# All output gates projected in the mixing stage, modulation rows turned as they come, and two buffers for high parts of weights

## What is computed

```python
mod = silu(c) @ ada_w + ada_b                    # 6 x 1024 per sequence: sh1, sc1, gt1, sh2, sc2, gt2
h = rms(x, norm1_w) * (1 + sc1) + sh1
proj = h @ w_in                                  # inputs, output gates g_z h_g s_z m_o, and 4 x 1024 gates
out_a = rms(gated_delta(g_qkv, ...)) * silu(g_z)   # branch A, width 256, and its new states
out_b = rms(hgrn2(h_q, h_f, h_i, ...)) * silu(h_g)
out_c = rms(ssd(s_xbc, s_dt, ...) * silu(s_z))
out_d = rms(mlstm(m_q, m_k, m_v, ...)) * sigmoid(m_o)
x = x + gt1 * (sum over branches n of sigmoid(gate_n) * (out_n @ w_branch_n)) @ w_out
x = x + gt2 * swiglu(rms(x, norm2_w) * (1 + sc2) + sh2)
y = rms(x, final_norm_w)
```

## Time and profile before

| what | value |
|---|---|
| median of 3 runs | 1264.69 us (1263.65 to 1268.71) |
| the profiled execution's own time | 1261.61 us |
| its span, first to last instruction | 1259.8 us |
| TensorE busy | 1166.7 us, 93% |
| VectorE busy | 576.5 us, 46% |
| ScalarE busy | 397.4 us, 32% |
| mean granted TensorE clock | 0.955 |
| moved by DMA | 116.76 MB, mean 93 GB/s |

### The profile page before, as it was taken

The page is one execution under the profiler, slowest core; times in us unless marked ns, Lnnn a source line. Parts: engine busy times, 40 slices in busy tenths (PEclk is TensorE's granted clock), DMA queues, the critical chain, the costliest instruction groups (busy, mean ns, idle before and its releaser), DMA issues. The chain is left out here.

```text
span 1259.8 us, 26885 instructions
## 1 busy us (share of the span) xinstructions
PE 1166.7 (93%) x11789; PEld 1091.8 (87%) x11789; DVE 576.5 (46%) x1054; ACT 397.4 (32%) x545; POOL 11.6 (1%) x29
## 2 busy tenths in 40 slices
PE   5679889999998898999999999959999999999997
PEld 3478888887767788999999998959999999999996
DVE  1365877678668663433333345452222222453322
ACT  1344383741102215932222221152232322341121
POOL 0000110000000000000000000000000000000000
PEclk9779999999779888999999999979999999999998
DMA  9802621122466306263333221213233232233301
GB/s 303 272 3 68 121 70 35 36 69 86 153 202 167 74 3 154 70 132 105 84 84 86 82 89 49 68 34 101 68 99 91 75 100 58 67 96 88 93 1 72
DMA packets 191034, 116.76 MB, mean 93 GB/s; under 512 B 36650, under 2 KB 189351, under 8 KB 190678
## 3 DMA queue, kind: packets, MB, share of 16 engines
q1 hardware_dynamic: 190358, 115.16, 32.8%
q0 software_dynamic: 576, 0.14, 0.1%
HBM read 108.31 MB, written 6.96 MB: 92 GB/s over the span
## 5 line engine op out<-in xcount | busy, mean ns | idle before, releaser
L833 PE MATMUL ps<-high_parts,scr_parts 128*128 128x272 f32 x2848 | 551.8, 293 | 16.7 <-DVE hT_parts L2765 7.9
L833 PEld LDWEIGHTS ps<-high_parts,scr_parts 128*128 128x128 f32 x2848 | 454.5, 191 | 20.1 <-issue 8.7
L833 PE MATMUL ps<-hT_parts,scr_parts 128*128 128x272 f32 x1488 | 414.2, 291 | 0.0
L2662 DVE TENSOR_TENSOR scr_parts<-ring,scr_parts 128x1024 fp32r<-128x1024 f32 (+1 forms) x104 | 133.7, 1286 | 331.4 <-ACT scr_parts L1826 328.2
L833 PEld LDWEIGHTS ps<-hT_parts,scr_parts 128*128 128x128 f32 x1488 | 276.9, 190 | 0.0
L1826 ACT ACTIVATE scr_parts<-ring 128x1024 fp32r<-128x1024 f32 (+1 forms) x104 | 115.2, 1109 | 467.4 <-PE ps L833 467.0
L833 PE MATMUL ps<-pj_parts,scr_parts 128*128 128x272 f32 x992 | 166.5, 292 | 2.1 <-DVEq L1966 1.8
L833 PE MATMUL ps<-high_parts,wx_hi 128*128 128x272 f32 x416 | 130.9, 315 | 20.4 <-DVE hT_parts L2035 7.3
L833 PEld LDWEIGHTS ps<-pj_parts,scr_parts 128*128 128x128 f32 x992 | 140.5, 188 | 3.6 <-DVEq L1966 2.2
L833 PE MATMUL ps<-high_parts,ring_parts 128*128 128x272 f32 x416 | 124.0, 298 | 0.0
L833 PE MATMUL ps<-hT_parts,wx_hi 128*128 128x272 f32 x416 | 123.9, 298 | 0.0
(11 more groups left out here) (326 smaller groups left out, 1060.9 us busy)
## 6 DMA issues: line engine op xcount, KB each, us to landing
ring<-in_w_in_dram SPq DMA_DIRECT2D x62, 512.0 KB, 5.5
ring<-in_ada_w_dram SPq DMA_DIRECT2D x48, 512.0 KB, 6.6
ring<-in_ffn_w_in_dram SPq DMA_DIRECT2D x44, 512.0 KB, 5.1
ring<-in_ffn_w_out_dram SPq DMA_DIRECT2D x16, 384.0 KB, 3.6
ring<-in_ffn_w_out_dram SPq DMA_DIRECT2D x16, 320.0 KB, 4.1
ring<-in_w_out_dram SPq DMA_DIRECT2D x8, 512.0 KB, 6.2
x_scratch<-scr SPq DMA_DIRECT2D x1, 2176.0 KB, 13.6
scr<-x_scratch SPq DMA_DIRECT2D x1, 2176.0 KB, 14.8
```

The costliest lines, as they stand in the source:

```text
L833: return pe.matmul(out, lhsT, rhs, start=start, stop=stop, skip_group_check=True)
L2662: dve.tensor_tensor(lo, src, hi.bitcast(F32), SUB).then_inc(w_split, 1)
```

## The change

- Groups 3 and 7 go into the mixing order, which ends 8, 3, 7, 14; `Z_ORDER` is empty, so `M_GATE` is 0 and the projection stage begins with the gate pieces. The tiles of group 3 wait in the plan for gdn's last sample state, those of group 7 for hgrn's, and in `read_group` for their write-outs. Lifting starts at piece 8 instead of 12.
- The first four gate loads wait for the four late groups, the others for the split of the piece that held their slot.
- Tiles with an odd number, but not the last, put their high parts into `pj[MO]`, `pj[MO + 1]` (the place of the last group's result); a copy then waits for the tile two back.
- A block of modulation rows is turned as soon as it has been copied: blocks 0 and 1 behind rounds 4 and 6 of the start loop, 2 and 3 behind the loop. `turn1` keeps the vectors' two transposes and comes ahead of `rs1`.
- `normalise_samples` uses two operations over all sequences instead of 16 (both norms).
- ScalarE makes all Silu gates and the Sigmoid of `m_o` in one row at the start of the projection stage; its loop there is written for gate pieces alone.

```diff
-MIX_ORDER += [8, 14]
-Z_ORDER = [3, 7]
+MIX_ORDER += [8, 3, 7, 14]
+Z_ORDER = []
...
-            need = ("hi", split, e) if side else ("half", split - 1, e)
+            need = ("hi", split, e) if side else ("half", split - (1 if split == len(mix_tiles) - 1 else 2), e)
...
                 needs.append(("lo", v, part_ // 2))
+                if v >= EARLY and MIX_ORDER[v // 2] in (3, 7):
+                    needs.append(("g", NT, "g_statec") if MIX_ORDER[v // 2] == 3 else ("h", NT, "h_statec"))
...
+        last_tile = 2 * len(MIX_ORDER) - 1
+
+        def mix_hi(i, e):
+
+            b = wx_hi[:, e, :] if i % 2 == 0 or i == last_tile else pj_parts[:, MO + e, 0:512]
+            return b.rearrange("p (k c) -> p k c", c=P)
...
-        pre += [("rs1", "act"), ("turn1", "pe"), ("mod1", "dve"), ("norm1", "act")]
+        pre += [("turn1", "pe"), ("rs1", "act"), ("mod1", "dve"), ("norm1", "act")]
...
-                if idx < 2:
+                if idx < R:
                     sp.wait_ge(x_done, TILE_DONE[EARLY + 2 * idx + 1])
                 else:
-                    sp.wait_ge(w_split, 2 * idx - 2)
+                    sp.wait_ge(w_split, 2 * (idx - R) + 2)
...
+            def turn_rows(b):
+
+                pe.wait_ge(rows_out, b + 1)
+                for c in range(4 * b, 4 * b + 4):
+                    mm(ps[:, 2, c * 9:(c + 1) * 9], ada_rows[:, c * P:(c + 1) * P], sum_groups)
...
                 last.then_inc(pre_s, 1)
+                if d in (4, 6):
+                    turn_rows(d // 2 - 2)
+            turn_rows(2)
+            turn_rows(3)
+            pe.wait_ge(d_vec, 16 * 17)
             pre.begin(pe, 0, "turn1")
-            pe.wait_ge(d_vec, 16 * 17)
             tr(ps[:, 1, 0:V_1], vrow[0:V_1, 0, :])
-            tr(ps[:, 1, V_1:V_2], vrow[0:V_2 - V_1, 1, :])
-            for c in range(16):
-                last = mm(ps[:, 0, c * 9:(c + 1) * 9], ada_rows[:, c * P:(c + 1) * P], sum_groups)
-            last.then_inc(pre_s, 1)
+            tr(ps[:, 1, V_1:V_2], vrow[0:V_2 - V_1, 1, :]).then_inc(pre_s, 1)
...
-                if i and e == 0:
-                    act.wait_ge(x_half, i)
-                elif i:
-                    act.wait_ge(x_done, TILE_DONE[i - 1])
-                act.activation(mix_hi(e), raw, ACT.Copy).then_inc(x_split_hi, 1)
+                user = i - 1 if i == last_tile else i - 2
+                if user >= 0 and e == 0:
+                    act.wait_ge(x_half, user + 1)
+                elif user >= 0:
+                    act.wait_ge(x_done, TILE_DONE[user])
+                act.activation(mix_hi(i, e), raw, ACT.Copy).then_inc(x_split_hi, 1)
...
-                    if f == SZ:
-
-                        act.wait_ge(q_out["ssd"], 128)
+                    if f in (SZ, GZ, HG):
+
+                        act.wait_ge(*{SZ: (q_out["ssd"], 128), GZ: (q_out["gdn"], 64), HG: (q_out["hgrn"], 64)}[f])
...
-            for z in (SZ, SZ + 1):
+            act.drain()
+            for z in (SZ, SZ + 1, GZ, GZ + 1, HG, HG + 1):
                 act.activation(pj[:, z, :], pj[:, z, :], ACT.Silu).then_inc(z_ready, 1)
-            act.drain()
             for z in (MO, MO + 1):
                 act.activation(pj[:, z, :], pj[:, z, :], ACT.Sigmoid).then_inc(z_ready, 1)
-            for m in range(M_GATE + 2):
+            for m in range(6):
                 n = m - 2
                 high(m + 2)
-                if m < M_GATE:
-                    z_out(m)
-                else:
-                    gate_out(m - M_GATE)
+                if m == GBUF.index(SB):
+
+                    act.wait_ge(q_out["mlstm"], 64)
+                gate_out(m)
                 if n >= 0:
                     mid.begin(act, 0, f"o_rs{n}")
...
-            for k in range(3, 4 * KD):
-                if k == GBUF.index(SB):
-
-                    act.wait_ge(q_out["mlstm"], 64)
+
+            for k in range(6, 4 * KD):
+                high(k + 2)
                 if k == len(GBUF):
 
                     act.wait_ge(branch_ready, 1)
-                high(M_GATE + k + 2)
                 gate_out(k)
...
-                for b in range(NB):
-                    c = slice(ND * b, ND * b + ND)
-                    dve.tensor_tensor(hs[:, :, c], hs[:, :, c], coef[:, :, 1 + b:2 + b].to_broadcast([P, KD, ND]), MUL)
-                dve.drain()
-                for b in range(NB):
-                    c = slice(ND * b, ND * b + ND)
-                    dve.tensor_tensor(hs[:, :, c], hs[:, :, c], mod[:, c0:c0 + KD, 1 + b:2 + b].to_broadcast([P, KD, ND]), ADD)
+                tt(h4, h4, coef[:, :, 1:9].unsqueeze(3).to_broadcast([P, KD, NB, ND]), MUL)
+                dve.tensor_tensor(h4, h4, mod[:, c0:c0 + KD, 1:9].unsqueeze(3).to_broadcast([P, KD, NB, ND]), ADD)
...
-                low(n + 7)
+                if n + 7 <= LAG:
+                    low(n + 7)
...
-                    dve.wait_ge(z_ready, (6, 8, 2, 4)[n])
+                    dve.wait_ge(z_ready, (4, 6, 2, 8)[n])
...
-            low(11)
-            low(12)
```

More of the change, by code:

```diff
@@ L285, in shared_order @@
     for e in range(2):
-        when[("lo", 0, e)] = 0.0
+        when[("lo", 0, e)] = when[("half", -1, e)] = 0.0
     left = {c: sum(cost(name, eng, t) + 0.1 for t, name, eng in stages) for c, stages in chains.items()}
@@ L469, in mix_weights @@
             return (b[:, n % R, :].rearrange("p (k c) -> p k c", k=KD)[:, 4 * e:4 * e + 4, c * P:(c + 1) * P] for b in (ring, ring_parts))
-        def mix_hi(e):
-            return wx_hi[:, e, :].rearrange("p (k c) -> p k c", c=P)
+        last_tile = 2 * len(MIX_ORDER) - 1
+        def mix_hi(i, e):
+            b = wx_hi[:, e, :] if i % 2 == 0 or i == last_tile else pj_parts[:, MO + e, 0:512]
+            return b.rearrange("p (k c) -> p k c", c=P)
         m_hi = [pj_parts[:, f, :] for f in MERGED_HI]
@@ L537, in trunk @@
         high_done = sem("high_done")
-        z_ready = sem("z_ready")
+        z_ready, rows_out = sem("z_ready"), sem("rows_out")
         q_out = {n: sem(f"q_out_{n}") for n in ("ssd", "gdn", "hgrn", "mlstm")}
@@ L681, in _ @@
             sp.dma_start(hrow[64:68, 0:NB * 5:5], A["state_mlstm_m"][0].rearrange("b h -> h b")).then_inc(d_st, 16)
-            loads = window + [("z", n) for n in range(counts["z"])]
+            loads = window
             for n in range(8, len(loads)):
@@ L897, in unit_part @@
                         pe.wait_ge(x_split, 2 * v + e + 1)
-                    wh, (_, wl) = mix_hi(e), mix_weights(v, e)
+                    wh, (_, wl) = mix_hi(v, e), mix_weights(v, e)
                     for k in range(4 * e, 4 * e + 4):
@@ L1637, in ada_out @@
             def ada_out(b):
-                act.activation(ada_rows[:, b * 512:(b + 1) * 512], ps[:, (2, 3, 6, 7)[b], :], ACT.Copy)
+                act.activation(ada_rows[:, b * 512:(b + 1) * 512], ps[:, (2, 3, 6, 7)[b], :], ACT.Copy).then_inc(rows_out, 1)
             for d in range(KD):
@@ L1832, in _ @@
             high(1)
-            def z_out(m):
-                act.wait_ge(w_done, m + 1)
-                act.wait_ge(q_out[("gdn", "hgrn")[m // 2]], 64)
-                act.activation(two(pj[:, Z_TILES[m], :]), ps[:, 2 * (m % 2):2 * (m % 2) + 2, 0:HN], ACT.Copy).then_inc(gate_read, 1)
             def gate_out(k):
@@ L1872, in _ @@
             act.drain()
-            high(M_GATE + 4)
-            gate_out(2)
-            for z in (GZ, GZ + 1, HG, HG + 1):
-                act.activation(pj[:, z, :], pj[:, z, :], ACT.Silu).then_inc(z_ready, 1)
-            for k in range(3, 4 * KD):
-                if k == GBUF.index(SB):
-                    act.wait_ge(q_out["mlstm"], 64)
+            for k in range(6, 4 * KD):
+                high(k + 2)
                 if k == len(GBUF):
                     act.wait_ge(branch_ready, 1)
-                high(M_GATE + k + 2)
                 gate_out(k)
@@ L1988, in _ @@
                 dve.wait_ge(x_split_hi, e + 1)
-                dve.tensor_tensor(lo, raw, mix_hi(e).bitcast(F32), SUB).then_inc(x_split, 1)
+                dve.tensor_tensor(lo, raw, mix_hi(0, e).bitcast(F32), SUB).then_inc(x_split, 1)
             pre.begin(dve, 0, "mod1")
             cp(vt[:, :], ps[:, 1, 0:V_2])
-            tt(mod[:, 0:16, :], ps[:, 0, 0:144].rearrange("p (c b) -> p c b", b=9), ada_bias(0, 16), ADD)
+            tt(mod[:, 0:16, :], ps[:, 2, 0:144].rearrange("p (c b) -> p c b", b=9), ada_bias(0, 16), ADD)
             done(pre)
@@ L2022, in weights_low @@
                 dve.wait_ge(x_split_hi, 2 * i + e + 1)
-                dve.tensor_tensor(lo, raw, mix_hi(e).bitcast(F32), SUB).then_inc(x_split, 1)
+                dve.tensor_tensor(lo, raw, mix_hi(i, e).bitcast(F32), SUB).then_inc(x_split, 1)
             coefficients(V_N1, 0)
```

## The result

The kernel after takes 1250.41 us (median of 4 runs, 1248.51 to 1253.88); beside it on the same chip the kernel before took 1266.7 us. The recorded ratio is 0.9884, with a 95% interval of 0.9851 to 0.9916; it is not the quotient of the two medians, which is 0.987. The prediction was 1255.0 (1247 to 1263), faster.

A forecast was written before the change was run, and what follows sets the result against it. TensorE, busy 93% of the span, was taken as the bound. Terms -1.3 - 1.9 - 6 - 2 + 1 - 0.9 - 1.4 + 2.8 = -9.7 us from 1261.6 gave 1251.9, stated as 1255.0 against the median; range 1247 to 1263.

The forecast's parts named there:

- the held read: Mixing stage: ScalarE's read, held 9.5 us until the SSD state left `pj`, still costs TensorE some 6 us.
- The second high buffer: Tiles from 84 to 165 us: removes five waits for low parts, gaining 6 us of 7.0, bounds 3.5 and 7.0.
- The two moved groups: Mixing stage: four added tiles fill waits for VectorE, 2 us won (0 to 9); lower clock costs 1 us.
- the step between the stages: Mixing to projection stage: tiles come last, so the 3.7 us wait shrinks to 2.8, 0.9 us won (0 to 1).
- The restart: First 8 us of the projection stage: half the 2.7 us cold start goes, 1.4 us won (0 to 2.7).
- ScalarE in the first pieces: Projection stage: gated norm rounds stall 0.65 us and a late gate read 2.1 us, 2.8 us lost (0 to 5).
- one load fewer: Rival, norm rounds: Ln and Exp share one table load, so the 0.65 us stall goes; 1254 us, chance 0.02.
- The turned rows: Start: turning modulation rows earlier brings `mod1` from 55.69 to near 54.3, 1.3 us won (1.7 gained to 2 lost).
- The samples' norm: Both norms: two operations replace sixteen small ones, 0.94 us each on the path, 1.9 us won (1.5 to 2.0).
- no change: Rival: ScalarE's and VectorE's orders bind, split waits return as read waits, moved tiles fill nothing; 1263 us, chance 0.22.
- Slower: Rival, chain stage: TensorE stays at 1.2 GHz while the added tiles run, +24 us; 1279 us, chance 0.06.
- Much faster: Rival: late tiles also cover the held read, 6.1 us, and a 2.7 us read wait; 1246 us, chance 0.08.

The follow-up runs named there:

- both edits of VectorE's and SP's order: Kernel after with each gate product right behind its scaling on VectorE and the SSD write-outs issued before the first late mixer load on SP: 1242.26 us, 0.9828.
- turned-rows-behind run: Kernel after with the groups in the projection stage again and all modulation rows turned behind the sums and `rs1`: 1248.18 us, 0.9885.

## Why the prediction was right, and where its steps were not

The outcome was as forecast: faster, 1250.4 in a range of 1247 to 1263. The sum was 3 to 5 us short. It priced the buffer too low and the loss by the moved groups too low as well, and the one partly hid the other: that the total came so near is in part luck. Of the signs given beforehand, the split waits gone, the one idle time near piece 8 and the held read still there (4.6 us for 6) came true, and none of the signs of being wrong; but `mod1` came at 52.6 for 54.3 and the last tile was read at 481.5, not near 490.

- **The second high buffer, 6 predicted, 11.6 measured by the times, 8 to 10 by the traces.** All 7.0 us of the split waits went, as the mechanism had it. The step that failed is "Gain 6 us of the 7.0": it took only the waits that name `ring_parts`, only the stretch from 84 to 165 us, and the order of the work as given. The order changed with the buffer. TensorE has 36 matmuls instead of 24 ahead of the small weights (a wait of 1.27 us for 3.41), and a further 2 us of idle time left the stretch from 165 us to the end of the stage, against which the lower clock took back about as much; the last 2.4 lay in the clock of the first pieces. How much of the whole the waits are worth without the other order stays open.
- **The two moved groups, -2 + 1 - 0.9 predicted.** The traces give 0 to 1.5 us won in the mixing stage for all three. The step that failed is that four more tiles fill the 3.2 us of waits for VectorE: four tiles run behind the last chain step, at clock 1.00, so neither the 2 us nor the 1 us of lower clock is there. Right was that the held read stays (9.43 us on ScalarE; 4.6 on TensorE) and that the step between the stages shrinks, 3.7 to 2.7; but it does so with the second buffer alone too, so it isn't the move's.
- **The restart, 1.4 predicted.** The first 8 us ran at 0.79 in both traces: 8 x (0.79 - 0.66) = 1.0 us. The kernel after with the groups in the projection stage has 0.79 too, and the moved groups alone and the second buffer alone have 1.00 each, so this isn't shown to be the move's.
- **ScalarE in the first pieces, +2.8 predicted, 3.5 measured**: stalls of 0.95 and 2.54 us for 0.65 and 2.1, at the two named places, with the named causes. What the step left out is the clock behind the second stall, 1.7 us more. So the term is 5.2, and it makes the move a loss: with it the prediction's terms for the move, which added up to 0.5 us won, would have been 1.9 lost. The Trainium skill, "ScalarE: Activation LUTs", section "Table sets: the hidden batching unit", holds that Ln then Exp needs one load. The start of the kernel after shows a load of 1.28 us between the two (48.69), and the first stall came, so the measurement speaks against that rule here, and the rival "one load fewer" with it. With the rule of the same section that calls are to be batched by set the trace agrees: a gated round of 8.37 us has three loads in it, 3.8 us.
- **The turned rows, 1.3 predicted, 3.1 at `mod1`.** The step that was off is "+2.0 us on its path": a round of the loop with a block in it takes 4.20 us for 3.63, so each of the two costs 0.57, and the last two blocks take 1.85 for 2.0. TensorE's work ended at 47.9 instead of 49.5, and the lower clock that the other bound assumed was not there.
- **The samples' norm, 1.9 predicted**: 0.96 at the first norm and 0.9 at the second.

Of the rivals, "no change" assumed that the orders of ScalarE and VectorE bind: not so, since the buffer alone gives 11.6 us; the case in which the planner keeps every copy in its old place did not come either. "Slower" needed 77 matmuls of the added tiles at half speed: the clock from 388 to 484 us was 0.95, where it had been 0.91 from 388 to 476 before. "Much faster" (the late tiles cover the held read) did not happen: TensorE waits 4.6 us for it.

One thing stays open. From first lift to the second norm's first operation the kernels with the moved groups and the write-outs in their old place take 265.14 to 265.17 us (six traces, the kernel after twice among them), all seven traces with the groups in the projection stage 263.63 to 263.65. The 1.5 us lie 200 us behind the first lift, where TensorE has an idle time of 1.8 us in both kinds: in the next 10 us the clock is 0.83 in the former and 1.00 in the latter. The kernel with both edits of VectorE's and SP's order keeps 1.00 there though its groups are moved, and takes 262.64. That makes the move's loss by the traces 5.5 + 1.5 - up to 1.5, for the 5 by the times; what decides the clock at this place, no run tells apart.

## What to carry to other kernels

A second buffer takes more away than the waits that name it, where the order of the work is planned by it: look for the other waits in the same stretch before pricing it, and build the old order with the new buffer if the two have to be told apart. Work that is moved off the busiest engine's stage to fill gaps elsewhere wins only what the gaps are, and nothing if it ends up behind the work with the gaps; it also takes away cover where it stood, so price the stalls that it uncovers with the clock that follows them. A stall removed ahead of a chain of dependent steps need not come back whole: here 3.1 and 3.6 us of it gave 1.3 and 3.5, each in one pair of traces. And a sum that must give the measured total checks nothing: ask for each part from a second pair of runs.

## What the runs showed that was not expected

**The same idle time, three clocks.** TensorE's idle time ahead of the projection's first piece is 2.69 us in the kernel after and in both kernels below, and what follows differs. First rows of the stage, in the turned-rows-behind run with the groups in the projection stage, and with the second buffer alone:

```profile
476.05 0.82 PE L836 MATMUL ps<-high_parts,scr_parts 128*128 128x272 f32 x2 [2.69 <-DVE scr_parts L2661]
```
```profile
468.15 0.52 PE L836 MATMUL ps<-high_parts,scr_parts 128*128 128x272 f32 x2 [2.69 <-DVE scr_parts L2666]
```

The windows of the first 8 us, in the same order:

```profile
476.05:484.05 8.00, 8.00 (x42) 8.00 (x43) 1.08 (x1) 4.62 (x6) 0.00 (x0) 0.62 1.19 292
```
```profile
468.15:476.15 8.00, 8.00 (x63) 8.00 (x64) 1.58 (x2) 6.20 (x8) 0.00 (x0) 1.00 1.19 292
```

Clock 0.62 in the one and 1.00 in the other, 0.79 in the kernel after: up to 3 us from an equal gap. A cost of a restart is a range, not a number.

**The scatter of one kernel is its clock.** Seven executions of the turned-rows-behind run span 1244.0 us at a mean clock of 0.962 to 1259.4 us at 0.949. Span times clock is 1196.7 and 1195.2: 15.4 us of span, 1.5 of work. In the trace of the latter TensorE ran at 0.76 from 303 to 404 us, where the kernel beside it had 0.86 from 303 to 390. So what a small edit wins has to be read from landmarks ahead of 180 us, which agree to 0.6 and to 1.4 us in the two pairs of traces of one kernel, or inside a stretch of equal clock.
